# First block, w_in and attention stage: the low halves of ten weight units per layer move from VectorE to GpSimd, and eight modulation units move one or two places later

## What is computed

```
mod = c_act @ w_ada + b_ada                     # six vectors of 1024
sh1, sc1, g1, sh2, sc2, g2 = split(mod, 6)
h = rmsnorm(x, norm1_w) * (1 + sc1) + sh1
u = h @ w_in                                    # 1024 x 5632
y_pool, y_conv, y_attn = windows(u), short_conv(u), attention(norm_rope(q), norm_rope(k), v)
x = x + g1 * (gated sum of the three @ w_out)
h2 = rmsnorm(x, norm2_w) * (1 + sc2) + sh2
x = x + g2 * ((silu(h2 @ w_gate) * (h2 @ w_up)) @ w_down)
```

## Time and profile before

| | us |
|---|---|
| median of 3 runs | 1790.68 (1789.91 to 1792.0) |
| the profiled execution | 1792.9 |
| its span in the profile | 1791.1 |
| PE busy | 1581.9 (88%) |
| DVE busy | 937.9 (52%) |
| ACT busy | 619.2 (35%) |
| POOL busy | 49.5 (3%) |
| mean granted clock of TensorE | 0.938 |

### The profile page before, as it was taken

How to read it: one execution, slowest core, us unless ns; L and a number is a source line. 1 busy time by engine, 2 the same in 40 slices (tenths; PEclk the granted TensorE clock), 3 DMA queues, 4 the chain that set the end, 5 groups by cost and what they waited for, 6 DMA issues and landing times.

```text
span 1791.1 us, 18861 instructions
## 1 busy us (share of the span) xinstructions
PE 1581.9 (88%) x7463; PEld 1086.6 (61%) x7463; DVE 937.9 (52%) x1402; ACT 619.2 (35%) x881; POOL 49.5 (3%) x66
## 2 busy tenths in 40 slices
PE   2889988999898998999979995999996996799985
PEld 1667866888677776788868873333335885433331
DVE  4897567775578657764456665110006675311102
ACT  2344534433344453443425651111114562111111
POOL 2000000000000000000030200000000010000000
PEclk8899999999999999999989896999998988899998
DMA  9576434986467634565645324999994416499994
GB/s 340 195 272 222 141 118 154 316 272 221 164 232 264 208 118 142 178 233 157 241 114 205 118 106 177 388 409 409 409 394 155 154 48 255 197 409 409 408 409 189
DMA packets 149963, 427.65 MB, mean 239 GB/s; under 512 B 8104, under 2 KB 16544, under 8 KB 149872
## 3 DMA queue, kind: packets, MB, share of 16 engines
q1 hardware_dynamic: 146192, 417.43, 63.6%
q0 software_dynamic: 3456, 8.87, 1.8%
q10 hardware_dynamic: 224, 0.07, 0.0%
HBM read 425.30 MB, written 1.05 MB: 238 GB/s over the span
## 4 chain that ended last, share of the span: by engine, by line
PE 63%; DVE 18%; SPq 6%; DMA 5%; ACT 4%; issue 4%; DVEq 0%; ACTq 0%
PE gp L2170 27%; PE gp L2559 9%; PE gp L2378 8%; SPq L734 6%; PE gp L2578 4%; DVE wlo L1322 4%; PE mp L2599 2%; DMA raw_more<-in_exp_w_up 2%; PE gp L2544 2%; ACT whi L842 2%; DVE acc L1232 1%; DVE ft L1373 1%; DMA raw<-in_w_ada 1%; DMA raw<-in_w_in 1%; PE mp L2201 1%
## 5 line engine op out<-in xcount | busy, mean ns | idle before, releaser
L1322 DVE TENSOR_TENSOR wlo<-raw,whi 128x2048 fp32r<-128x2048 f32 (+1 forms) x132 | 289.5, 2194 | 209.7 <-ACT whi L842 206.8
L842 ACT ACTIVATE whi<-raw 128x2048 fp32r<-128x2048 f32 (+1 forms) x132 | 241.5, 1834 | 322.7 <-PE gp L2170 182.6
L2170 PE MATMUL gp<-whi,xt_hi 128*128 128x512 f32 (+1 forms) x800 | 319.1, 399 | 24.6 <-DVE xt_lo L1383 15.1
L2170 PE MATMUL gp<-wlo,xt_hi 128*128 128x512 f32 (+1 forms) x800 | 311.3, 389 | 0.0
L2170 PE MATMUL gp<-whi,xt_lo 128*128 128x512 f32 (+1 forms) x800 | 310.6, 388 | 0.0
L2170 PEld LDWEIGHTS gp<-whi,xt_hi 128*128 128x128 f32 x800 | 154.6, 193 | 67.4 <-issue 16.7
L2170 PEld LDWEIGHTS gp<-whi,xt_lo 128*128 128x128 f32 x800 | 154.4, 193 | 31.2
L2170 PEld LDWEIGHTS gp<-wlo,xt_hi 128*128 128x128 f32 x800 | 154.5, 193 | 29.4 <-issue 1.0
L2037 DVE TENSOR_SCALAR pr<-slots,key,dg 128x128 f32<-128x128 f32 x64 | 19.3, 344 | 260.6 <-PE gp L2589 260.6
L2378 PE MATMUL gp<-whi,xt_hi 128*128 128x512 f32 (+1 forms) x224 | 85.3, 381 | 5.3 <-DVE xt_lo L1757 3.1
L1232 DVE SCALAR_TENSOR_TENSOR acc<-raw,cact,acc 128x1024 f32<-128x1024 f32 x69 | 88.5, 1282 | 2.3 <-DMA raw<-in_w_ada 0.9
(11 more groups left out here) (390 smaller groups left out, 2358.4 us busy)
## 6 DMA issues: line engine op xcount, KB each, us to landing
raw<-in_w_in SPq DMA_DIRECT2D x60, 1024.0 KB, 5.4
raw<-in_w_ada SPq DMA_DIRECT2D x42, 1024.0 KB, 5.3
raw_deep<-in_exp_w_down SPq DMA_DIRECT2D x36, 1024.0 KB, 17.0
raw_deep<-in_exp_w_gate SPq DMA_DIRECT2D x30, 1024.0 KB, 14.5
raw_deep<-in_exp_w_up SPq DMA_DIRECT2D x30, 1024.0 KB, 16.7
raw<-in_w_gate SPq DMA_DIRECT2D x20, 1024.0 KB, 5.1
raw<-in_w_up SPq DMA_DIRECT2D x20, 1024.0 KB, 5.1
raw<-in_w_down SPq DMA_DIRECT2D x20, 1024.0 KB, 5.0
```

What stands on the lines that cost most here:

```text
L842: act.activation(slot(whi, s % SPLIT, units, cols), slot(raw, g % RAW, units, cols), ACT.Copy).then_inc(hi_done.sem, 1)
L1322: dve.tensor_tensor(slot(wlo, s % SPLIT, units, cols), slot(raw, g % RAW, units, cols), slot(whi, s % SPLIT, units, cols).bitcast(F32), AL ...
L2170: mm = pe.matmul(gp[:, q % 2, t, 0:wide], a[:, chunk, ts], w[:, unit, c0:c0 + wide], start=first and n == 0 and m == 0, stop=last and n == ...
```

## The change

A table `POOL_LOW` names the units 3, 5, ..., 21 of each layer of the first block. Their low halves are subtracted by GpSimd, which has the ten of a layer in a row in its list, behind the two bias loads of that layer; VectorE leaves them out, and does the other units as before. `NORM_AT` moves: modulation units 12 to 18 stand one unit later, and unit 19 two units later (behind unit 18, in front of which it used to stand behind 16). The slots, the number of loads and all arithmetic stay.

```diff
-NORM_AT = (9, 10, 11, 12, 13, 14, 15, 16)
+NORM_AT = (10, 11, 12, 13, 14, 15, 16, 18)
+POOL_LOW = range(3, S_BR, 2)
...
+                for s in POOL_LOW:
+                    g = G_OF["split", s]
+                    _, units, cols = weights(("split", s), l)
+
+                    pool.wait_ge(*hi_done.at(l, s + 1))
+                    pool.tensor_tensor(slot(wlo, s % SPLIT, units, cols), slot(raw, g % RAW, units, cols),
+                                       slot(whi, s % SPLIT, units, cols).bitcast(F32), ALU.subtract).then_inc(raw_read[g % RAW].sem, 1)
...
-                    dve.wait_ge(*hi_done.at(l, s + 1))
-                    dve.tensor_tensor(slot(wlo, s % SPLIT, units, cols), slot(raw, g % RAW, units, cols),
-                                      slot(whi, s % SPLIT, units, cols).bitcast(F32), ALU.subtract).then_inc(raw_read[g % RAW].sem, 1)
+                    if s not in POOL_LOW:
+                        dve.wait_ge(*hi_done.at(l, s + 1))
+                        dve.tensor_tensor(slot(wlo, s % SPLIT, units, cols), slot(raw, g % RAW, units, cols),
+                                          slot(whi, s % SPLIT, units, cols).bitcast(F32), ALU.subtract).then_inc(raw_read[g % RAW].sem, 1)
```

## The result

| | before | changed |
|---|---|---|
| median of the runs, us | 1791.34 (1789.91 to 1792.06, 4 runs) | 1818.43 (1816.68 to 1820.43, 4 runs) |
| span of the profiled execution, us | 1791.1 | 1815.8 |
| first and second layer's stage, us | 161.28, 160.55 | 176.04, 173.18 |
| mean granted clock | 0.938 | 0.935 |

The ratio is 1.0153, with an interval of 1.0137 to 1.0168: slower by 27.1 us, where 17.0 were forecast. The direction is right; the time lies 1.4 us above the range. "The stage" is here the time from TensorE's first product of w_in to the sum of the modulation vectors, as in the earlier trace rows. The two stages grew by 14.8 and 12.6 us, together 27.4, so the loss is all there.

A forecast was written before the change was run, and what follows sets the result against it. TensorE was busy for 88% of the span, with VectorE's list the bound in front of `grow`. 8.2 + 3 + 5.8 = +17.0 us; against the median of 1790.68 that gave 1807.7 us, range 1776 to 1817.

The forecast's parts named there:

- The price of a subtraction: 2.2 us on VectorE, 4.56 on GpSimd, which holds VectorE's instructions with two SBUF inputs for its whole length.
- The first rival: VectorE is not held by odd units in front of `grow`; waits go, sum -15.8 us, 1774.9 us; chance 0.26.
- The second rival: VectorE and GpSimd take turns within instructions; VectorE loses about what it saves: -6 to +3, near 1789 us; chance 0.10.
- A: Way to the update of `grow` in both layers: work moved off VectorE, holds, pauses, late slots; +4.8 and +3.4, sum +8.2 us.
- hold term: In front of `grow`, five GpSimd subtractions, 22.8 us less 5.5 covered by other VectorE work, hold VectorE 17.3 us per layer.
- pauses and late slots: In front of `grow`: pause of 1.85 (second layer 3.29) goes; late slots cost 0 to 11.8, taken as 3 us per layer.
- B: At `weigh(0)`, head 1's softmax starts 1.0 to 2.3 us later behind unit 15 on GpSimd; 1.5 per layer, +3 us.
- C: At `weigh(3)`, modulation unit 19 joins the chain, +2.6, and the windows start later, +0.3: +2.9 per layer, +5.8 us.
- likeliest range: The likeliest case's own range, 1799 to 1817 us: no late slots and B's lower end, to half their upper end.
- At nothing: Second layer's bias loads behind ten GpSimd subtractions, later loads behind twenty, cost nothing; feed-forward and second block shift whole.
- The third rival: The ring of three slots becomes the bound: late slots cost 11.8 us instead of 3 per layer, 1825 us; chance 0.04.

The follow-up runs named there:

- experiments 3 to 5: Changed kernel with GpSimd's subtraction replaced, in order, by one zero fill (1770.70 us), two and a half fills (1783.52 us), a copy of `raw` (2362.21 us).
- Experiment 4: Changed kernel with GpSimd's subtraction replaced by a long fill: two and a half fills, then the slot given back; 1783.52 us, ratio 0.9968.
- late five: Only units 13, 15, 17, 19 and 21 subtracted on GpSimd, modulation units placed as in the kernel before; 1796.03 us, ratio 1.0031.
- experiment 1: Changed kernel's two parts apart: GpSimd's subtractions with modulation units at old places, 1808.73 us (1.0098); new places with all subtractions on VectorE, 1791.38 us (0.9999).
- experiment 7: Changed kernel with modulation unit 19 behind unit 19's place instead of unit 18's; 1804.19 us, ratio 1.0069.
- experiment 5: Changed kernel with GpSimd's subtraction replaced by a copy of `raw` into the low half; 2362.21 us, the second block taking another path through its experts.
- experiment 8: Against the changed kernel, only units 7, 16 on GpSimd, old modulation places: 1784.03 us; units 7, 16, 19, six modulation units moved: 1776.49, repeated 1775.29 us.
- no subtraction: Changed kernel with the ten subtractions per layer left out on every engine, low halves of odd units stale; 1772.36 us, ratio 0.9898.

## Why the forecast missed its size

**The price of a subtraction: right, and shown.** In layer 1 four instructions read longer by 4.3 each, the reduction did not, and by experiments 3 to 5 it is GpSimd's read that counts. The rule of the Trainium skill (SBUF — State Buffer, "Who interferes with whom") holds here in each point that these runs touch: the fill that only writes held nothing, and the reduction kept its length. One of the four is the TENSOR_SCALAR of a modulation unit, which the prediction counted among those that read two tensors in SBUF; it reads one. The first rival (no hold, 1774.9) falls; its first layer was also added up wrongly, since its terms give -9.2 and not -11.2, so it should have stood at 1776.9. The long fill is the nearest thing to it that was measured, VectorE relieved and not held but everything as late: 1783.5. Lateness cost more than the 1 us a layer that this rival gave it. The second rival falls too, turns within an instruction: the held rows are one full wait plus one full length.

**A, the way to `grow`: forecast +4.8 and +3.4, measured +7.2 and +4.4.** The hold term was 17.3 us, and the rows of layer 1 give 17.3, which is luck: the three copies shortened no hold, and a pause and the reduction covered a whole unit. The term that was mis-sized is that of the pauses and late slots: I let the pause of 1.85 go and put 3 us in its place. VectorE's idle time between 71 and 133 us is 1.57 + 1.53 + 1.85 + 0.33 = 5.3 us, each ended by ScalarE. 5.3 instead of 3 is 2.3, the whole miss in that layer (7.15 - 4.8). In layer 2 two misses hide each other. VectorE's rows there:

```profile
526.82 4.49 DVE L1331 TENSOR_TENSOR wlo<-raw,whi 128x2048 fp32r<-128x2048 f32 x1 [1.53 <-ACT whi L850]
537.71 5.70 DVE L1240 SCALAR_TENSOR_TENSOR acc<-raw,cact,acc 128x1024 f32<-128x1024 f32 x2 [3.88 <-DMA raw<-in_w_ada]
559.50 4.28 DVE L1367 TENSOR_TENSOR rt<-rr 128x32 f32<-128x32 f32 x1
574.24 5.13 DVE L1472 TENSOR_TENSOR w<-u,cos 128x512 f32<-128x512 f32 x1
```

Less their own 2.29, 2.60, 0.19 and 0.69 they held 13.8 us, 3.5 less than the term. The pauses are 10.1 instead of 6.3 before, where the forecast had them 0.3 shorter; it had counted only one of the old ones, 3.29. Part of the new ones goes with a wait for GpSimd's low half of unit 7 that I had listed only under the first rival. Experiment 4 gives the cost of lateness by itself, 7.4 and 5.6 us, well inside the bounds of 0 to 11.8 and about twice what I took.

**B, `weigh(0)`: forecast +1.5 per layer, measured +1.7 and +2.5.** The mechanism is the one told; in layer 2 it is past the upper end of 2.3 given there. The late five alone show it without A and C. What B had wrong lies behind it, in the three steps that make up the row from `weigh(0)` to `weigh(3)`. In us, layer 1 and layer 2:

| from | to | before | changed |
|---|---|---|---|
| `weigh(0)` | `weigh(1)` | 10.10, 10.10 | 11.88, 10.77 |
| `weigh(1)` | `weigh(2)` | 9.12, 10.71 | 7.46, 7.48 |
| `weigh(2)` | `weigh(3)` | 7.79, 7.49 | 10.54, 11.67 |

Such a step takes 7.5 us without a wait and at the full clock. Behind the waits of `weigh(0)`, 3.22 and 4.04 us, it took 4.4 and 3.3 more; in layer 1 the granted clock is 0.50 from 167.0 to 170.5. The wait of `weigh(1)`, of which the prediction said that it stays, went with its own lower clock: in layer 1 `pt` was done at 176.8, and TensorE, slowed, came at 178.76. The two nearly cancel, so the row of the table above does not show them.

**C, `weigh(3)`: forecast +2.9 per layer, measured +5.9 and +5.8.** This is the step that failed. Its wait was right in layer 1 and 1.1 us short in layer 2: 2.91 and 4.02 us. (That the row from `weigh(0)` to `weigh(3)` grew by 2.9 in layer 1 as well is chance, as the three steps show.) What I put at nothing is what follows behind it, 3.0 and 4.1 us: the unit behind the new wait runs at the lower clock. The transposes behind the wait for `grow` showed the same thing with its price, 3.65 us at 0.50. I used it in the rival that takes a wait away, and not in the sum that adds one; only the upper end of the range had "some more time at the lower clock", some 3 us. The waits of `weigh(0)`, `weigh(1)` and `weigh(3)` taken together grew by 7.3 us over both layers (14.2 instead of 6.9), where B and C forecast 8.8; B and C together cost 15.9. That is also where the 5 us of experiment 1 come from that belong to neither part: from `weigh(0)` to the modulation sum both parts together cost 11.7 us, the subtractions alone -0.7 and the places alone 7.1. With the subtractions alone the wait at `weigh(3)` is 1.41 and 0.23 us and costs only itself (29.58 and 29.62 us behind it); with modulation unit 19 in front of head 4's softmax as well it is 2.91 and 4.02, and the unit behind it costs as much again.

The sum by places, in the rows of the first table: A 11.5, B 4.2, C 4.5 + 7.2, 27.4 us of stage. Of the 10.4 above the forecast's 17.0, 7.2 are the lower clock behind `weigh(3)`, 3.3 the pauses in A less the hold that was too large, 1.2 B, less 1.3 by which the row in front of `weigh(3)` grew less than C's wait was forecast. The foot of the likeliest range was off as well: its terms give 1800.7, not 1799.

**At nothing: held.** From the end of the first stage to the start of the second 279.7 us instead of 281.7, behind the second 1133.5 instead of 1135.2: the bias loads behind GpSimd's list delayed nothing. **The third rival** had the right direction for the slots but the wrong size; 1825 is 7 us too much, and by experiment 7 most of the miss is elsewhere. What stays open is why the lower clock followed some of the middling waits and not others (below), and how much of the lateness reaches TensorE by the ring of three and how much by `wlo` itself coming later; the long fill moves both.

## To carry over

Before work goes to an idle GpSimd, list what VectorE does in exactly those microseconds: an instruction with two inputs in SBUF, or a TENSOR_SCALAR from SBUF to SBUF, stands there for the rest of GpSimd's. So a unit is worth moving where it meets a reduction, work out of PSUM or a pause, as units 7 and 16 did here, or where nothing waits for what it holds, as with unit 19. Price each new wait of TensorE with what the clock does behind it, from a wait of like length that the trace already has. Do this for each wait on the way, since a wait that grows can swallow a later one, and two wrong terms can look like a right one. And change one place at a time, since a move that is free alone (the places, ratio 0.9999) cost more beside the other: 5 us by the stages, 10 by the medians.

## What was not expected of the hardware

A modulation instruction with one tensor in SBUF, the TENSOR_SCALAR at 120.53, was held too: 5.09 us beside GpSimd's row at 120.16, where it takes 0.75 alone (and 2.39 beside the copy of experiment 5). The step of the filters in experiment 8 is a second case. The Trainium skill (SBUF — State Buffer, "Who interferes with whom") does say that this operation can take a mode that uses the shared ports; the rows agree. The hold also goes the other way: unit 15's subtraction on GpSimd, at 157.41, began 0.05 us after a modulation instruction and reads 5.71 us instead of 4.6. At `weigh(3)`, where all versions do the same work, waits of up to 1.41 us were followed by 29.4 to 29.6 us to the modulation sum and waits of 2.82 to 4.02 us by 32.6 to 33.6; of three waits between them, the one of 1.84 us (no subtraction, layer 2) was followed by 31.2, and those of 1.86 and 1.87 (fill) by 29.6. At `weigh(1)` of the kernel before, waits of 2.34 and 2.36 us were followed by steps of 9.12 and 10.71 us instead of 7.5. So a short wait is cheap, a long one costs about double, and in between it isn't settled by its length alone. And the fills on GpSimd, of 128x2048 in 1.81 us, lengthened neither VectorE's subtractions (2.29) nor its modulation instructions (1283 ns) in the runs with 20 and with 40 of them.
